# A mixture of experts in items of 32 tokens on four column tiles, and three serial chains of other stages taken apart

## The chip, the cores and the metric

The kernel runs on one core of a Trainium2 chip. The metric is the time of one execution on the device, in microseconds (us); lower is better. All data is float32.

Words used here: PE is TensorE (PEld its weight loads), DVE is VectorE, ACT is ScalarE, POOL is GpSimd, SP is SyncE, which here only issues transfers (DMA). A *bank* is one of the eight accumulators of TensorE, 128 rows of 512 float32. A *column tile* is a strip of TensorE's columns that works on a stationary matrix of 64 or 32 columns and writes its own rows of a bank; two strips of 64 or four of 32 lie side by side.

## What is computed

Three networks in a row, on 256 tokens of width 1024. The part of most interest here is the mixture of experts at the end of the first. Each token goes to 4 of 32 experts; every expert has three matrices of 1024 x 1024 (gate, up and down, 4 MB each):

```python
def moe(h, w_router, b_router, w_gate, b_gate, w_up, b_up, w_down, b_down):
...
    top_logit, top_idx = lax.top_k(logits, TOP_K)
    gates = jax.nn.softmax(top_logit, axis=-1)
...
    def expert_block(args):
        xb, e = args
        g = jnp.minimum(xb @ w_gate[e] + b_gate[e], SWIGLU_LIMIT)
        u = jnp.clip(xb @ w_up[e] + b_up[e], -SWIGLU_LIMIT, SWIGLU_LIMIT)
        act = g * jax.nn.sigmoid(SWIGLU_ALPHA * g) * (u + 1)
        return act @ w_down[e] + b_down[e]
```

The reference's router gives the experts, on the inputs used, these numbers of tokens: 24, 33, 24, 34, 36, 4, 13, 32, 47, 47, 52, 21, 25, 51, 33, 13, 27, 58, 22, 29, 73, 9, 35, 41, 25, 35, 39, 38, 34, 20, 14, 36.

The second network is a hybrid layer (three branches, a convolution among them whose channels are layer-normed, and merge gates):

```python
    cv = jax.nn.silu(layer_norm(causal_depthwise_conv(glu, conv_w, conv_b), cv_ln_g, cv_ln_b))
...
    gates = jax.nn.sigmoid(merge.reshape(B, S, N_BRANCH, D))
```

The third has two layers of feed-forward network, mixer (a pooling in one, a differential attention in the other) and feed-forward network. The attention ends in

```python
    o = sweep_query_blocks(block, q)
    o = rms_norm_3(o, subln_g) * (1 - lam_init)
    return o.reshape(b, s, d) @ w_o
```

with `o` of 8 heads of 128.

## The kernel before

Stages follow one another: `mla`, `route`, `experts_tiled` (268 to 1234 us of the span), `second` (to about 1612), and then in `third` the feed-forward networks `ffn`, `pool_mixer`, `ffn`, `ffn`, `diff_attention`, `ffn`, and a last norm. Within a stage every engine has its own instruction list, in the order in which the code is written; semaphores are all that ties them. No scheduler reorders anything.

**Route and experts.** `route` makes a list of *items*: an item is up to `SLOTS` (64) tokens of one expert. `weights_of[e]` is the expert of item e, `ends_of[x]` the number of items up to the end of expert x, `n_items` their sum. Both are read on the chip by `value_load`. An item goes through these steps on PE:

- `gather`: a 0/1 matrix `choice` (token by slot) picks the item's rows out of `h_rows`, into bank X; ACT copies them to `x_rows`; `turn` transposes them back into bank X, and ACT copies that to `xs`, features by slots.
- `gate_up`: `product` takes `xs` as the stationary matrix (128 x 64) and the weights as the moving one (128 x 512), the two halves of the output on two column tiles; gate goes into bank G, up into bank U. ACT copies each to rows (`g_rows`, `u_rows`), `turn` transposes each, DVE adds biases, limits, and multiplies, with a sigmoid of ACT's between, which gives `act_s`.
- `down`: the same product with `act_s`, into bank Y; ACT copies it to `ys`.
- `spreading` and `scatter`: a matrix of gates by slot (`gated`), transposed into `spread`, adds `ys` into the rows of the tokens in banks 0 to 3, which stay open over all items.

The steps of neighbouring items are interleaved: in turn e of the loop PE does gate_up(e), with gather(e+1) in its middle, then spreading and down of e-1, the turns of e+1, and scatter(e-1).

**Weights.** An expert's 12 MB lie in six tiles `raw0` to `raw5` of 2 MB (gate 0 and 1, up 2 and 3, down 4 and 5), of which there is only one set. SP runs through the experts: for each piece it waits until `used[p]` has reached `ends_of[e-1]`, which is when the last item of expert e-1 has gone over the piece, and issues the load (L1411). PE waits for `landed[p]`.

**Second.** `project(n)` is a loop of n turns of the projection of the stage's input by `w_in` (L1795), 64 matmuls a turn; the last three are for the merge gates, and ACT's `take` applies the sigmoid to what it leaves. PE sums the convolution's channels (a product with ones, L1869 for the squares, taken by ACT at L1951), and then attends (L1878, L1805) with the probabilities that ACT copies at L1964.

**SideSums.** Beside each feed-forward network, POOL fetches pieces of the modulation matrix `in_mod_w` and DVE sums them. POOL begins with a memset of `ffn_side_bias` (L337), its load (L333), and two loads of weights (L328). DVE starts the network with the norm's scaling (L437).

**Diff-attention's end.** DVE's `take_o` (L2866) copies head by head into `o` (16 blocks of 128 x 128, the tile `ring`). ACT squares all of `o` (L2800), DVE sums by head (L2885), ACT takes a root, DVE the reciprocal and 16 scalings (L2893), PE transposes (L2745), DVE copies four banks with the gain `subln` (L2898), and PE multiplies by `w_o` (L2755).

## Time and profile before

| | us |
|---|---|
| median of 3 runs | 2725.25 (2723.86 to 2725.43) |
| the profiled execution | 2726.04 |
| its span | 2724.4 |
| PE busy | 2519.5 (92%) |
| DVE, ACT, POOL busy | 1060.0, 369.6, 43.4 |
| moved by DMA | 728 MB, mean 267 GB/s |

The profile comes from one execution. "Busy" is the sum of the times in which an engine had an instruction in work. The *granted clock* is the share of TensorE's full clock that the chip gave it (1.00 is 2.4 GHz, 0.5 is 1.2 GHz). The DMA share is the mean busy share of the core's 16 DMA engines. In the rows below, the number in brackets at the end of a row is the time that the engine had stood before it, and behind the arrow what ended that.

The experts take 965 us, over a third of the time, and in them the DMA share is near 1 for most of the time. In the second and third network PE is busy nearly throughout.

### The profile page before, as it was taken

Reading aid. Unit: us, or ns where it says so; the run is one execution under the profiler, and the core shown is the slowest. Engines: PE = TensorE matmul, PEld = TensorE weight load, DVE = VectorE, ACT = ScalarE, POOL = GpSimd, SP = SyncE. Lnnn points to the kernel's source line nnn. Section 1 sums busy time; section 2 is a strip of 40 time slices with the busy share of each in tenths; the row PEclk is TensorE's granted clock in tenths of the full one; section 3 lists DMA queues with packets and bytes.
Section 4 is the critical chain, followed back from the end, with each engine's and each line's share of the span. In section 5 each row is a group of like instructions: output and inputs, shape, how many; then the busy total and the mean of one; then the engine's idle time right before and its main releaser. Section 6 shows DMA issues by size and latency. Waiting matters only on the chain. (4 is left out here: it accounts for less than half of the span.)

```text
span 2724.4 us, 33615 instructions
## 1 busy us (share of the span) xinstructions
PE 2519.5 (92%) x12943; PEld 1538.4 (56%) x12944; DVE 1060.0 (39%) x2210; ACT 369.6 (14%) x743; POOL 43.4 (2%) x64
## 2 busy tenths in 40 slices
PE   6998999999999799997999889998999999987998
PEld 2444333333333233336878758777876887855876
DVE  1233121121221121224381248746996443244433
ACT  2122111111111111111121210011002000131001
POOL 0000000000000000000000000000100000000000
PEclk8998999999999899998989999999999999998999
DMA  8603999999997799998434359754997553140443
GB/s 330 261 10 138 427 429 428 428 429 428 428 429 334 336 429 429 428 409 315 148 117 158 120 196 347 273 179 141 378 382 273 197 165 108 69 155 26 153 160 102
DMA packets 188019, 728.24 MB, mean 267 GB/s; under 512 B 9758, under 2 KB 103292, under 8 KB 159156
## 3 DMA queue, kind: packets, MB, share of 16 engines
q1 hardware_dynamic: 168324, 651.29, 61.2%
q0 software_dynamic: 19632, 76.09, 7.1%
q8 instruction: 43, 0.70, 0.1%
q14 instruction: 20, 0.16, 0.0%
HBM read 726.30 MB, written 1.05 MB: 267 GB/s over the span
## 5 line engine op out<-in xcount | busy, mean ns | idle before, releaser
L1496 PE MATMUL bank<-experts_raw,experts_xs 128*64 128x512 f32 x2112 | 472.7, 596 | 18.7 <-DMA experts_raw<-in_w_up 15.2
L1496 PEld LDWEIGHTS bank<-experts_raw,experts_xs 128*64 128x64 f32 x2112 | 147.0, 137 | 334.3 <-issue 289.3
L2379 PE MATMUL bank<-big,ffn_actT 128*128 128x512 f32 x704 | 309.1, 592 | 0.0
L1496 PE MATMUL bank<-experts_raw,tiled_act_s 128*64 128x512 f32 x1056 | 241.4, 602 | 52.1 <-DMA experts_raw<-in_w_down 50.8
L1795 PE MATMUL bank<-hT,ring 128*128 128x256 f32 x1024 | 224.7, 383 | 3.2 <-DMA ring<-in_w_in 2.1
L1795 PEld LDWEIGHTS bank<-hT,ring 128*128 128x128 f32 x1024 | 196.6, 192 | 32.1 <-issue 5.0
L2379 PEld LDWEIGHTS bank<-big,ffn_actT 128*128 128x128 f32 x704 | 130.5, 190 | 148.3 <-issue 148.3
L1630 DVE COPY tiled_spread<-bank 128x256 f32<-128x256 f32 x33 | 14.0, 425 | 441.2 <-PE bank L1532 441.2
L1496 PEld LDWEIGHTS bank<-experts_raw,tiled_act_s 128*64 128x64 f32 x1056 | 71.3, 138 | 200.3 <-issue 123.2
L2254 PEld LDWEIGHTS bank<-hT,big 128*128 128x128 f32 x1408 | 165.2, 193 | 18.3 <-issue 18.3
L2254 PE MATMUL bank<-hT,big 128*128 128x128 f32 x1408 | 166.3, 277 | 0.0
L296 DVE SCALAR_TENSOR_TENSOR layer_sums<-ring,cact,layer_sums 128x512 f32 (+1 forms) x210 | 140.5, 747 | 0.8 <-DMA ring<-in_mod_w 0.8
L1661 DVE TENSOR_TENSOR tiled_up<-bank,tiled_cur 128x512 f32<-128x512 f32 x33 | 22.8, 692 | 256.2 <-PE bank L1516 256.2
L2254 PE MATMUL bank<-big,ffn_sums_of_weights 128*128 128x128 f32 x1056 | 121.9, 275 | 0.2 <-DVE ffn_sums_of_weights L2221 0.2
L2254 PE MATMUL bank<-big,ring 128*128 128x128 f32 x1056 | 121.5, 275 | 0.0
L2254 PEld LDWEIGHTS bank<-big,ffn_sums_of_weights 128*128 128x128 f32 x1056 | 119.8, 192 | 0.4 <-issue 0.4
L2254 PEld LDWEIGHTS bank<-big,ring 128*128 128x128 f32 x1056 | 119.7, 192 | 0.0
L2273 DVE TENSOR_TENSOR ring<-ffn_gu,bank 128x256 f32<-128x256 f32 x22 | 9.3, 422 | 226.2 <-PE bank L2254 226.2
L2254 PE MATMUL bank<-big 128*128 128x128 f32 x704 | 85.9, 275 | 0.0
L2439 ACT ACTIVATE ffn_gu<-ffn_gu 128x512 f32<-128x512 f32 x44 | 27.8, 632 | 408.2 <-DVE ffn_gu L2273 408.2
L2254 PEld LDWEIGHTS bank<-big 128*128 128x128 f32 x704 | 82.1, 192 | 0.0
L1542 PE MATMUL bank<-tiled_ys,tiled_spread 64*128 64x512 f32 x264 | 65.6, 615 | 0.8 <-ACT tiled_ys L1586 0.8
(479 smaller groups left out, 2645.1 us busy)
## 6 DMA issues: line engine op xcount, KB each, us to landing
experts_raw<-in_w_gate SPq DMA_DIRECT2D x64, 2048.0 KB, 23.7
experts_raw<-in_w_up SPq DMA_DIRECT2D x64, 2048.0 KB, 25.1
experts_raw<-in_w_down SPq DMA_DIRECT2D x64, 2048.0 KB, 25.5
big<-in_ffn_w_gu SPq DMA_DIRECT2D x88, 1024.0 KB, 9.5
ring<-in_mod_w POOLq DMA_DIRECT2D x30, 2048.0 KB, 10.8
big<-in_ffn_w_down SPq DMA_DIRECT2D x44, 1024.0 KB, 5.1
ring<-in_w_in SPq DMA_DIRECT2D x16, 2048.0 KB, 8.5
mla_wm<-in_w_mod SPq DMA_DIRECT2D x24, 1024.0 KB, 6.7
```

The source lines that it names most:

```text
L296: op = vec.scalar_tensor_tensor(dst[:, o], src[:, j, o], c[:, j:j + 1], dst[:, o], ALU.mult, ALU.add)
L1496: last = nc.tensor.matmul(bank[b][h * HALF:(h + 1) * HALF, :], stationary(kt), raw[p][:, k, h * C:(h + 1) * C], start=kt == 0, stop=kt == ...
L1542: op = nc.tensor.matmul(bank[2 * t + h][:], spread[rows, t * P:(t + 1) * P], ys[rows, :], start=False, stop=end)
L1630: vec.tensor_copy(spread[:], bank[X][:, 0:SEQ]).then_inc(spread_ready, 1)
L1661: vec.tensor_tensor(tiles(up), turned(U), wide(cur[:, KT:2 * KT]), ALU.add).then_inc(u_taken, 1)
L1795: last = nc.tensor.matmul(bank[b][:, (f % 2) * SEQ:(f % 2 + 1) * SEQ], w_k[s][:, k, f * P:(f + 1) * P], core.hT[:, k, :], start=k == 0, st ...
L2254: last = self.nc.tensor.matmul(core.bank[b][:, o:o + P], left(m, k), right(k), start=k == 0, stop=k == half - 1)
L2273: op = lambda o, x, y, f=ALU.add: vec.tensor_tensor(o, x, y, f)
L2379: last = nc.tensor.matmul(bank[b][:], actT[:, s, f, t * P:(t + 1) * P], wd[:, s, f, n * 512:(n + 1) * 512], start=start and f == 0, stop=s ...
L2439: nc.scalar.activation(gu[:, :, 0, :], gu[:, :, 0, :], ACT.Silu).then_inc(*silu_ready.up())
```

## The change

The number of slots in an item falls from 64 to 32, and four strips of TensorE's columns are used in place of two. Gate and up of one item now share bank G (gate's two halves and up's two halves are its four quarters), so one copy of ACT (`gu_rows`) and one `turn_gu` serve both. In `down` two strips take the even k and two the odd k of each half; the two partial sums lie in different rows of `ys`, and are added by `scatter`, whose matrix `gated` has each slot's gate twice. `gate_up` is called in halves of its k, and the order of the steps in the loop changes; the pieces are loaded in the order 0, 2, 1, 3, 4, 5. `route` counts up to eight items for an expert (columns of the table `row`) and clears the upper half of `x_rows` on POOL.

Outside the experts: in `second`, `project(3)` becomes `project(2)` before and `project(1)` behind the sums of L1869, and ACT's sigmoids are split in the same way. In `SideSums.gpsimd` the first two loads of weights go ahead of the memset, which waits for the network's norm. In `diff_attention` squares and sums are taken for heads 0 to 5 first and for 6 and 7 later; the scalings go by quarters of two heads, each of which frees PE's transposes; ACT makes the copies of DVE; and PE's product waits for each pair of features apart.

```diff
-SLOTS = 64
+SLOTS = 32
...
+        for s in range(2):
+            load(s, slice(self.first * PIECE, (self.first + 1) * PIECE))
+        if ready:
+            pool.wait_ge(*ready)
         if self.bias is not None:
             self.st.nc.gpsimd.memset(self.bias[:], 0.0).then_inc(*self.zeroed.up())
             pool.wait_ge(*self.zeroed.own())
         load_bias(slice(self.first * PIECE, (self.first + 1) * PIECE))
...
+    GATE_UP, DOWN = (0, 2, 1, 3), (4, 5)
...
-            load(1, 0)
-            load(1, 1)
-            with sp.Fori(2, E) as e:
-                load(e, 0)
-                load(e, 1)
-                load(e - 1, 2)
-            load(E - 1, 2)
+                for p in pieces:
+                    sp.wait_ge(used[p], last)
+                    weights.load(sp, which, p)
+
+            with sp.Fori(1, E) as e:
+                load(e, weights.GATE_UP + weights.DOWN)
...
+            def gate_up(e, *halves):
+                if 0 in halves:
+                    after(pe, xs_ready, e)
+                    after(pe, gu_copied, e)
+                expert = expert_at(pe, e)
+                for q in halves:
+                    for m in range(2):
+                        pe.wait_ge(landed[2 * m + q], 16 * expert + 16)
+                    for k in range(ROWS):
+                        kt = ROWS * q + k
+                        for m in range(2):
+                            for h in range(2):
+                                o = (2 * m + h) * SLOTS
+                                last = nc.tensor.matmul(bank[G][o:o + SLOTS, :], tiles(xs)[:, kt % 4, kt // 4, :],
+                                                        raw[2 * m + q][:, k, h * C:(h + 1) * C],
+                                                        start=kt == 0, stop=kt == KT - 1)
+                            if k == ROWS - 1:
+                                last.then_inc(used[2 * m + q], 1)
+
+            def down(e):
+                after(pe, act_ready, e + 1)
+                expert = expert_at(pe, e)
+                for q in range(2):
+                    pe.wait_ge(landed[4 + q], 16 * expert + 16)
                     for k in range(ROWS):
                         kt = ROWS * q + k
                         for h in range(2):
...
+                            o = (2 * h + k % 2) * SLOTS
+                            last = nc.tensor.matmul(bank[Y][o:o + SLOTS, :], tiles(act_s)[:, kt % 4, kt // 4, :],
+                                                    raw[4 + q][:, k, h * C:(h + 1) * C],
+                                                    start=kt < 2, stop=kt >= KT - 2)
+                    last.then_inc(used[4 + q], 1)
+
+            def turn_gu(e):
+                after(pe, gu_copied, e + 1)
                 after(pe, u_taken, e)
                 for j in range(4):
...
+                    last = nc.tensor.transpose(bank[T][:, j * P:(j + 1) * P], gu_rows[:, adjacent(j)], core.ident[:])
+                last.then_inc(gu_turned, 1)
...
             with pe.Fori(1, items) as e:
-                gate_up(e)
-                turn(e + 1, g_rows, g_copied, G, g_turned)
+
+                gate_up(e, 0)
+                down(e - 1)
+                gather(e + 1)
+                gate_up(e, 1)
                 spreading(e - 1, x_copied, e + 1)
-                down(e - 1)
+                turn_gu(e)
                 after(pe, spread_ready, e)
-                turn(e + 1, x_rows, x_copied, X, x_turned)
-                turn(e + 1, u_rows, u_copied, U, u_turned)
+                turn_x(e + 1)
                 scatter(e - 1)
...
             with act.Fori(1, items) as e:
+                take_y(e - 1)
                 take_gu(e)
-                take_y(e - 1)
...
-            project(3)
+            project(2)
             pe.wait_ge(*S["squared"].next(pe))
             core.claim(pe, 6)
             for j in range(4):
                 last = nc.tensor.matmul(bank[6][:, 0:SEQ], core.ones[:], glu[:, j, 0:SEQ],
                                         start=j == 0, stop=j == 3)
             last.then_inc(*core.filled[6].up())
+            project(1)
...
-            take(MERGE, 3, ACT.Sigmoid)
+            take(MERGE, 1, ACT.Sigmoid)
             act.wait_ge(*S["centred"].next(act, 4))
             run(glu[:, :, 0:SEQ], tiles(B_GLU), ACT.Square).then_inc(*S["squared"].up())
+            take(MERGE + 8, 1, ACT.Sigmoid)
             act.wait_ge(*S["chan_var"].next(act))
             run(chan[:, 0, :], chan[:, 1, :], ACT.Sqrt).then_inc(*S["chan_dev"].up())
             for j in range(4):
                 act.wait_ge(*S["scaled"].next(act))
                 run(tiles(B_GLU)[:, j, :], tiles(B_GLU)[:, j, :], ACT.Silu, scale=core.column("cv_ln_g_2", j),
                     bias=core.column("cv_ln_b_2", j)).then_inc(*S["cv_ready"].up())
+            take(MERGE + 16, 1, ACT.Sigmoid)
...
-                side.gpsimd(pool)
+                side.gpsimd(pool, norm.normed.next(pool, TT))
...
-            pe.wait_ge(*S["o_ready"].next(pe))
             for q in range(4):
+                pe.wait_ge(*S["o_ready"].next(pe))
...
+                        if b == 0 and k % 2 == 0:
+                            core.copied(pe, k // 2)
...
+            def squares(first, end):
+
+                for b in (6, 7):
+                    act.wait_ge(*core.emptied[b].ahead(TT + end // 2))
+                heads = slice(first * P, end * P)
+                run(junk[:, :, heads], o[:, :, heads], ACT.Square).then_inc(*S["o_sq"].up())
...
+                if h == H3 - 2:
+                    squares(0, H3 - 2)
             core.load_root(act)
-            act.wait_ge(*S["mixed"].next(act))
-            run(junk, o, ACT.Square).then_inc(*S["o_sq"].up())
+            squares(H3 - 2, H3)
...
+            for q in range(4):
+                core.filled[q].passed(act, 4)
+                act.wait_ge(*core.filled[q].next(act))
+                run(oT[:, 2 * q:2 * q + 2, :], bank[q][:].rearrange("p (f n) -> p f n", f=2), ACT.Copy, scale=subln[:])\
+                    .then_inc(*core.emptied[q].up())
...
+            sums(0, H3 - 2)
             take_o(H3 - 2)
             take_o(H3 - 1)
-            dve.wait_ge(*core.read(dve, 6))
-            dve.wait_ge(*core.read(dve, 7))
-            vec.tensor_copy(lam[:, 6:7], lam[:, 5:6]).then_inc(*S["mixed"].up())
-
-            dve.wait_ge(*S["o_sq"].next(dve))
-            heads = lambda a: a.rearrange("p t (h n) -> p t h n", h=H3)
-            then(vec.reduce_sum(ostat[:, 0, :].rearrange("p (t h) -> p t h", t=TT), heads(junk), AX))
+            sums(H3 - 2, H3)
+            for b in (6, 7):
+                dve.wait_ge(*core.read(dve, b))
             vec.tensor_scalar(ostat[:, 1, :], ostat[:, 0, :], 1.0 / P, RMS_EPS, ALU.mult, ALU.add)\
                 .then_inc(*S["o_mean"].up())
             dve.wait_ge(*S["o_root"].next(dve))
             then(vec.reciprocal(ostat[:, 3, :], ostat[:, 2, :]))
-            for t in range(TT):
-                for h in range(H3):
-                    i = t * H3 + h
-                    op = vec.tensor_scalar(o[:, t, h * P:(h + 1) * P], o[:, t, h * P:(h + 1) * P],
-                                           ostat[:, 3, i:i + 1], None, ALU.mult)
-            op.then_inc(*S["o_ready"].up())
             for q in range(4):
-                dve.wait_ge(*core.filled[q].next(dve))
-                vec.tensor_scalar(oT[:, 2 * q:2 * q + 2, :], bank[q][:].rearrange("p (f n) -> p f n", f=2),
-                                  subln[:], None, ALU.mult).then_inc(*core.emptied[q].up())
+                for h in (2 * q, 2 * q + 1):
+                    for t in range(TT):
+                        i = t * H3 + h
+                        op = vec.tensor_scalar(o[:, t, h * P:(h + 1) * P], o[:, t, h * P:(h + 1) * P],
+                                               ostat[:, 3, i:i + 1], None, ALU.mult)
+                op.then_inc(*S["o_ready"].up())
+                core.filled[q].passed(dve, 1)
```

Left out of the diff are the widths of tiles and tables that follow from `SLOTS`, the bank numbers, the code that `gate_up` and `down` replace, and the wait `mixed`, which is gone.

**PE's list, the loop over the items.** In the order's rows, `experts_xs` is `xs`, `experts_raw` the weights, TENSOR_LOAD and ISA belong to the reading of the item's expert. Before, from the gather in the middle of gate_up to the end of the turn:

```order
L1524 MATMUL bank<-experts_h_rows,experts_choice 64x512 x4
L1496 MATMUL bank<-experts_raw,experts_xs 64x512 x16
L1516 MATMUL bank<-ident,tiled_g_rows 128x128 x4
L1532 MATMUL bank<-ident,tiled_gated 128x128 x2
L1462 ISA
L1462 TENSOR_LOAD experts_weights_of
L1462 ISA x2
L1492 ISA
L1496 MATMUL bank<-experts_raw,tiled_act_s 64x512 x16
L1516 MATMUL bank<-ident,experts_x_rows 128x128 x4
L1516 MATMUL bank<-ident,tiled_u_rows 128x128 x4
L1542 MATMUL bank<-tiled_ys,tiled_spread 128x512 x4
```

After, from down(e-1) on, which now stands between the two halves of gate_up(e) (the first half is above these rows):

```order
L1522 ISA
L1527 MATMUL bank<-experts_raw,tiled_act_s 32x512 x16
L1468 REGISTER_ALU
L1550 MATMUL bank<-experts_h_rows,experts_choice 32x512 x4
L1475 TENSOR_LOAD experts_weights_of
L1475 ISA x2
L1506 ISA
L1512 MATMUL bank<-experts_raw,experts_xs 32x512 x16
L1558 MATMUL bank<-ident,tiled_gated 128x128 x2
L1536 MATMUL bank<-ident,tiled_gu_rows 128x128 x4
L1542 MATMUL bank<-ident,experts_x_rows 128x128 x4
L1568 MATMUL bank<-tiled_ys,tiled_spread 128x512 x4
```

Down(e-1) and the gather moved ahead of gate_up's second half, the turns of g and u became one, and spreading, turns and scatter are all that stands between the end of an item's gate_up and the next one's.

**SP's list, one turn of the loop over the experts.** Before, from the last gate piece on (the waits' registers are loaded by TENSOR_LOAD):

```order
L1411 DMA experts_raw<-in_w_gate 128x4096
L1469 TENSOR_LOAD experts_ends_of
L1469 ISA x2
L1411 DMA experts_raw<-in_w_up 128x4096 x2
L1469 ISA
L1469 TENSOR_LOAD experts_ends_of
L1469 ISA x2
L1411 ISA
L1411 DMA experts_raw<-in_w_down 128x4096
L1411 ISA
L1411 DMA experts_raw<-in_w_down 128x4096
```

After, the whole turn:

```order
L1491 ISA
L1482 TENSOR_LOAD experts_ends_of
L1482 ISA x2
L1425 ISA
L1425 DMA experts_raw<-in_w_gate 128x4096
L1425 DMA experts_raw<-in_w_up 128x4096
L1425 ISA
L1425 DMA experts_raw<-in_w_gate 128x4096
L1425 DMA experts_raw<-in_w_up 128x4096
L1425 DMA experts_raw<-in_w_down 128x4096 x2
```

Before, the down pieces of an expert were issued behind the gate and up pieces of the next one; now they are issued in their own expert's turn, and `ends_of` is read once a turn in place of three times.

**PE's list, the merge gates in the second network.** Before, from the last matmuls of project(3) on; `second_glu` is the squared convolution, `second_logit` the attention's probabilities:

```order
L1795 MATMUL bank<-hT,ring 128x256 x16
L102 REGISTER_ALU
L102 COMPARE_AND_BRANCH
L1869 MATMUL bank<-second_glu,ones 128x256 x4
L1878 MATMUL bank<-ident,second_logit 128x128 x8
L1805 MATMUL bank<-second_sg,big 128x256 x2
```

After:

```order
L1821 MATMUL bank<-hT,ring 128x256 x16
L102 REGISTER_ALU
L102 COMPARE_AND_BRANCH
L1895 MATMUL bank<-second_glu,ones 128x256 x4
L102 UNCONDITIONAL_BRANCH
L1821 MATMUL bank<-hT,ring 128x256 x64
L102 REGISTER_ALU
L102 COMPARE_AND_BRANCH
L1905 MATMUL bank<-ident,second_logit 128x128 x8
L1831 MATMUL bank<-second_sg,big 128x256 x2
```

A third of the projection (the row of 64 matmuls, between its branches) moved from ahead of L1869 to behind it, now L1895, and ahead of the first transposes of the attention, now L1905.

## Rows read from the trace of the kernel before

**Rows 1.** Table of windows, the experts' stage; columns in its first line.

```profile
core 0: us, PE busy (x) PEld busy (x) DVE busy (x) ACT busy (x) POOL busy (x), PEclk, DMA share, GB/s
300.00:850.00 550.00, 514.96 (x2404) 182.90 (x2404) 113.02 (x342) 69.39 (x115) 0.00 (x0) 1.00 1.01 428
850.00:900.00 50.00, 33.70 (x160) 11.97 (x156) 7.91 (x23) 4.85 (x8) 0.00 (x0) 0.89 0.72 300
900.00:1000.00 100.00, 98.97 (x458) 36.05 (x460) 21.83 (x67) 12.05 (x20) 0.00 (x0) 0.97 0.86 366
...
1190.00:1235.00 45.00, 38.46 (x176) 13.09 (x172) 9.88 (x25) 6.89 (x14) 0.00 (x0) 1.00 0.97 391
```

**Rows 2.** The page's costliest groups: busy us, mean ns, idle before.

```profile
L1496 PE MATMUL bank<-experts_raw,experts_xs 128*64 128x512 f32 x2112 | 472.7, 596 | 18.7 <-DMA experts_raw<-in_w_up 15.2
...
L2254 PE MATMUL bank<-hT,big 128*128 128x128 f32 x1408 | 166.3, 277 | 0.0
```

**Rows 3.** Timeline (start, us, what), PE, at products on four column tiles.

```profile
73.78 1.92 PE L569 MATMUL bank<-mla_wm,first_cpad 128*32 128x512 f32 x16
75.64 7.17 PE L778 MATMUL bank<-mla_win,mla_ctx_hT 128*128 128x256 f32 x32
```

**Rows 4.** Timeline at expert 20, the one with two items.

```profile
873.18 3.76 SPq L1411 DMA_DIRECT2D experts_raw<-in_w_gate  x2
...
876.26 1.89 PE L1524 MATMUL bank<-experts_h_rows,experts_choice 128*64 128x512 f32 x8
...
877.98 7.04 PE L1496 MATMUL bank<-experts_raw,experts_xs 128*64 128x512 f32 x32
...
901.03 9.36 PE L1496 MATMUL bank<-experts_raw,tiled_act_s 128*64 128x512 f32 x32 [15.12 <-DMA experts_raw<-in_w_down]
...
910.32 0.75 PE L1516 MATMUL bank<-ident,experts_x_rows 128*128 128x128 f32 x4
...
911.48 1.99 PE L1542 MATMUL bank<-tiled_ys,tiled_spread 64*128 64x512 f32 x8
...
913.40 7.09 PE L1496 MATMUL bank<-experts_raw,experts_xs 128*64 128x512 f32 x32
```

**Rows 5.** Transfers, KB each and us to landing: issued 873 to 874; whole span.

```profile
experts_raw<-in_w_gate SPq DMA_DIRECT2D x1, 2048.0 KB, 8.3
...
experts_raw<-in_w_down SPq DMA_DIRECT2D x64, 2048.0 KB, 25.5
```

**Rows 6.** Timeline, the end of the experts.

```profile
1227.68 3.65 PE L1496 MATMUL bank<-experts_raw,tiled_act_s 128*64 128x512 f32 x16 [1.33 <-DMA experts_raw<-in_w_down]
...
1232.12 1.99 PE L1542 MATMUL bank<-tiled_ys,tiled_spread 64*128 64x512 f32 x8 [0.79 <-ACT tiled_ys L1586]
```

**Rows 7.** Second network: the projection's group, then the timeline at its two waits.

```profile
L1795 PE MATMUL bank<-hT,ring 128*128 128x256 f32 x1024 | 224.7, 383 | 3.2 <-DMA ring<-in_w_in 2.1
...
1514.61 1.99 PE L1869 MATMUL bank<-second_glu,ones 128*128 128x256 f32 x8 [2.03 <-ACT second_glu L1951]
...
1522.60 2.07 PE L1805 MATMUL bank<-second_sg,big 128*128 128x256 f32 x4 [5.12 <-ACT second_sg L1964]
```

**Rows 8.** Timeline at the start of two feed-forward networks.

```profile
1613.50 2.51 DVE L437 TENSOR_SCALAR big<-x,ffn_small 128x1024 f32<-128x1024 f32 x2
1613.84 0.97 POOL L337 MEMSET ffn_side_bias<- 128x1024 f32 x1
...
2497.83 1.42 DVE L437 TENSOR_SCALAR big<-x,ffn_small 128x1024 f32<-128x1024 f32 x2
```

**Rows 9.** Timeline, the end of the differential attention.

```profile
2453.31 0.42 DVE L2866 COPY ring<-bank 128x256 f32<-128x256 f32 x1 [0.47 <-PE bank L2724]
...
2455.97 2.29 DVE L2885 TENSOR_REDUCE diff_ostat<-diff_weights_wqk 128x16 f32<-128x2048 f32 x1 [1.98 <-ACT diff_weights_wqk L2800]
...
2459.03 3.22 DVE L2893 TENSOR_SCALAR ring<-ring,diff_ostat 128x128 f32<-128x128 f32 x16
2462.31 3.52 PE L2745 MATMUL bank<-ident,ring 128*128 128x128 f32 x16 [9.04 <-DVE ring L2893]
...
2466.99 3.24 PE L2755 MATMUL bank<-diff_weights_wqk,hT 128*128 128x512 f32 x7 [1.15 <-DVE hT L2898]
```

More of the change, by code:

```diff
@@ L339, in gpsimd @@
         load_bias(slice(self.first * PIECE, (self.first + 1) * PIECE))
-        for s in range(2):
-            load(s, slice(self.first * PIECE, (self.first + 1) * PIECE))
         with turns(pool, self.n_pieces - 1, *[(x, 1) for x in self.loads + self.w_used]) as i:
@@ L1308, in _ @@
             act.wait_ge(*core.filled[7].next(act))
-            run(item.xs[:], core.bank[7][:], ACT.Copy).then_inc(*core.emptied[7].up())
+            run(item.xs[:].rearrange("p (j c) -> p j c", j=4), item.rows_of(core.bank[7]), ACT.Copy).then_inc(*core.emptied[7].up())
         @block.vector
```

140 lines of the change are left out of this document (64 added, 76 removed).

## Prediction

> **What bounds the kernel now.** The profiled execution took 2726.04 us (span 2724.4); the median of the runs shown is 2725.25, so a sum made on the profiled one stands 0.8 us high, which I leave in. I read first the table of windows over the experts. From 300 to 850 the DMA share is 1.01 at 428 GB/s, with PE busy 515 of 550 us [rows 1]: the transfers of the experts' weights set the pace, and PE fits in under them. One 2 MB piece at 429 GB/s takes 4.89 us, an expert's six take 29.35. The share falls in two places: 300 and 366 GB/s in 850 to 1000, which is (1 - 300/429) x 50 + (1 - 366/429) x 100 = 15.0 + 14.7 us of flow lost, and 391 in the last window, 4.0 us [rows 1]. **33.7 us of flow are lost in all.** So every change to the experts has to be read as lost flow, not as PE time. The timeline around 870 to 925 says why. That expert (number 20, 73 tokens) is the only one with two items of 64 slots. A piece is loaded again only when the expert's last item has used it, so from 873.18 the queue starts empty and the first piece lands 8.3 us after its issue, against some 25 in the steady stream [rows 4, 5]: 8.27 - 4.89 = 3.4 us of start, and PE then stood 15.12 us for the down weights [rows 4].
>
> With one item of about 26.6 us (three products of 32 matmuls, 7.04 to 7.09 us each, a gather of 1.89, three turns of up to 0.75 and a scatter of 1.99 [rows 4], which overlap by a tenth or two where they meet) against 29.35 us of flow, PE waits 2 to 3 us per expert. That is all a faster item can find there, and it isn't on the path.
>
> **Part 1, the experts: the items.** From the reference's routing the tokens per expert are known; in items of 64 that is 33, which the 2112 matmuls of L1496 for gate and up confirm (64 an item [rows 2]). In items of 32 it is **50: 15 experts of one item, 16 of two, one of three.** What is an exception before, the expert whose weights may only be reloaded after a second pass, becomes every second expert. This is what I cost.
>
> *An item's PE time.* Four column tiles in place of two: if the four run together, a product of 64 matmuls takes the time that 32 instructions take now. L1496 goes at 7.04 us per 16 steps of two halves, 0.43 us a step. Four tiles of 32 columns exist at L569: 16 instructions in 1.92 us, the next group starting 1.86 later [rows 3], 0.43 to 0.46 us for each four. So gate and up together 2 x 3.43 us (two steps of four for each of the eight k, halved by piece pairs), down 3.43, gather 1.7, spread 0.4, two turns 0.6 each, scatter 1.9 (the rows of [rows 4] less the overlap), with about 0.9 of waiting for ACT's one copy of gate and up (0.60 us of copy and its signals) and no work between to hide it: **16.0 us against 26.6.** The last stretch, spread, wait, turns and scatter, is 4.1 of them.
>
> *One-item experts.* 16.0 us of PE against 29.35 of flow: PE now stands for about 12 us in each, and they stay at the pace of the DMA. The one cost I see is the clock. After the 15.12 us of standing, the next 32 matmuls took 9.36 us instead of 7.04 [rows 4], and the granted clock of that window is 0.89 instead of 1.00 [rows 1]: 11 us at half clock (1.2 GHz against 2.4). In the new order down(e-1) stands behind gate_up(e, 0), so the down pieces are handed back only 3.4 + 3.4 us after p0 and p2 of the next expert land; the flow of p1 and p3, 9.78 us, covers 9.78 - 3.38 of start - 0.4 of issue - 5.15 until the first half of down is through = 0.85 us. Half clock takes 2.3 us more (9.36 - 7.04), and about 1.4 lie open: **15 x 1.4 = 20.6 us (from 0 to 21).**
>
> *Two-item experts.* The loop that closes is: the second item's gate_up first half ends and gives p0 and p2 back; SP issues (0.4); the queue being empty by then, p0 lands after 8.27 [rows 5]; p2, p1, p3 follow at 4.89 each; the next expert's gate_up second half runs (3.43), its tail (4.1), and the second item's first half again (3.43). 0.4 + 8.27 + 14.68 + 3.43 + 4.1 + 3.43 = 34.3 us, 34.2 with the overlaps of the issue. That is **4.84 over 29.35** where two-item experts follow each other, 4.43 where they follow a one-item expert; 15 that aren't the last of the row, 69.7 us. The two down pieces are issued within that time and land by 33.1 of the 34.3, so they don't lengthen it; they are why the queue is empty when p0 is asked for. The three-item expert adds a whole item, 16.0 + 4.5 = 20.5.
>
> *Sum.* Lost flow 69.7 + 20.6 + 20.5 = 110.8, against 33.7 before: +77.1. After the last piece lands, before: 1227.68 to about 1234, 6.3 us (the 3.65 us of down and a scatter of 1.99 [rows 6]). After, expert 31 has two items, and the last piece can land only before the first's down: half a down, gather, gate_up second half, tail, then down of the second and its scatter (1.7 + 1.7 + 3.4 + 4.1 + 3.4 + 0.8 for the copy + 2.0 = 17.1), with 2.3 for half clock and some 0.5 where PE reads the expert's number: about 19.9, or +13.6. I take **+90.4** for the experts (90.7 by these terms, less the 0.3 of narrower copies in route).
>
> Both ends of what the trace doesn't show: the step of a quad is 0.43 by L569 in runs of 16; in runs of 16 steps back to back no row shows it. The nearest row on short instructions is L2254, 1408 in 166.3 us [rows 2], 0.118 us for each pair of weight load and matmul, so 0.47 us for four pairs against 0.43: a tenth more on 13 us of an item gives 1.3 us, of which the loop holds 6.9 us' worth of matmul (0.69) and the tail some: +16 in all. I keep 0.43, since the nearest row in form is L569, and carry the 16 as an end. From an empty queue the landing took 8.27; between 7.5 and 9.0, 16 restarts move the sum from 70 to 105. The switches between tile shapes get fewer, less than 0.2 us an item.
>
> [...]
>
> **Part 2, outside the experts.** *Second:* the merge gate's projection is cut in three and laid into the waits of its chain. PE waited 2.03 us before L1869 and 5.12 before L1805, for ACT's square and for the copy behind its table loads and Silus [rows 7]. Now ACT squares after the first of three sigmoids, while PE is at the second third of the projection, and the last third, 64 matmuls of 0.22 us or 14 us [rows 7], stands where PE waited 5.12. It was done anyway, and covers either wait. ACT changes its table more often, beside those projections. I take 7.4: 2.03 + 5.12, and 0.25 for the half clock that a wait of 5 us leaves behind (L1805's first four in 2.07 us [rows 7]), from 6 to 9. *SideSums:* the bias memset waits for the norm, so L437 at 1613.50 no longer shares its port: 2.51 us for two against 1.42 at 2497.83 [rows 8]: 1.1 us, once, since only here a memset of 0.97 fell on it. Behind the waiting memset on POOL stand the bias load and the later turns of weights, not the first two, which now go ahead of it; the bias, which VectorE needs with the first weights, comes a microsecond or two later and is small beside their 2 MB. *Diff-attention:* from the end of the last copy, 2453.73, to the first L2755 at 2466.99 there are 13.3 us [rows 9]: a square over all heads (about 1.9), a reduction of 2.29, 16 scalings of 3.22, 16 transposes of 3.52, four copies that end 0.4 before. After: a quarter of square and sum (0.5 + 0.65), root and reciprocal (0.8), then scalings, transposes and ACT copies in four interleaved quarters, the scalings setting the pace at 0.8 each, L2755 after the first two quarters. It starts at about 2460.6, 6.4 earlier, but waits once more per pair of banks and begins at the low clock: **5 (3.4 to 6.5).** Sum of part 2: 7.4 + 1.1 + 5.0 = **13.5 less (9 to 16).**
>
> **Forecast:** 2726.0 + 90.4 - 13.5 = 2802.9, **2803 us.**
>
> **The rivals.** *A, half clock costs nothing.* For: the products are half as long, so the half clock may be over sooner for each, and 0.85 us are covered. Against: 9.36 in place of 7.04 after one wait [rows 4]. 2803 - 20.6 = 2782. *B, slower quads.* Four tiles in long runs at 0.47 us, by L2254's pace: 2803 + 16 = 2819; for it, a quad in 0.43 us leaves 0.107 for each weight load with its matmul, and L2254 takes 0.118 [rows 2]; against it, L569 does it, in runs of 16 [rows 3]. *C, the other side: the loads never run dry.* If SP's issue for p0 comes while p5 is still in flight, the 3.4 of start are hidden, and if the loop closes in 29.35, two-item experts cost nothing. Then 2726.0 - 33.7 + 20.5 + 13.6 - 13.5 = 2713, faster by 13. It decides from 29.35: my loop has 34.3, and 30.9 even with the start hidden, so PE's share of it (10.96 us) would have to be under 9.4 as well. For: each of the loop's terms has been timed elsewhere than in such a loop, and most could only come out shorter. Against: at 873.18 it did start empty [rows 4, 5]. *D, the change doesn't do what it says:* quads that run as pairs make an item 26.5 us and two-item experts 53 us; over 3100. L569 speaks against it [rows 3].
>
> **How the numbers follow.** Forecast 0.60 (2790 to 2815, its unknown landing time and part 2), A 0.13, B 0.17, C 0.05, D 0.02, the remaining 0.03 for a loss I haven't seen that stops at about 2730. The range takes in A and B with the ends of the landing time: **2772 to 2832.** A measurement of this kernel can tell about 0.2% (5.5 us). Faster by more: C, 0.05. Within: 0.02. Slower: 0.93.
>
> **What would show it.** In the profile after: items in x50; DMA share 1.0 over a row of one-item experts and about 0.86 (29.35/34.2) over two-item experts; gate loads landing 8 to 9 us after issue in the latter; PE's largest idle group under L1512 waiting for gate or up, some 12 us an expert, with PEclk at 0.8 or 0.9 across the stage; the experts' last scatter about 90 us later. L569's pace in L1512: 16 matmuls in 1.9 us. In second no wait over 1 us before L1895 and L1831; in diff-attention L2785 some 6 us after the last copy. I'm wrong if the DMA share stays at 1.0 over two-item experts (C), if the loop's length isn't 34 us, or if PEclk stays at 1.0 with the one-item experts at 29.35 (A).

## The result

The changed kernel takes **2803.96 us** (median of 4 runs, 2799.70 to 2808.41), the kernel before 2724.56 (4 runs, 2722.70 to 2725.43): a ratio of **1.0294, with an interval of 1.0276 to 1.0313**. That is 79.4 us slower, where 2803 was forecast. The profiled execution of the changed kernel took 2799.7 us, 73.7 more than the profiled one of before (2726.04).

The table of windows of the changed kernel, columns as in [rows 1], for the long stretch of the experts, for two one-item experts (434 to 495) and for one expert of two items that follows another such (537 to 572):

```profile
300.00:1190.00 890.00, 695.70 (x5178) 295.27 (x5170) 195.68 (x765) 105.75 (x214) 0.00 (x0) 0.91 0.91 377
```

```profile
537.00:572.00 35.00, 32.31 (x255) 14.92 (x251) 9.18 (x36) 4.95 (x10) 0.00 (x0) 1.00 0.86 360
...
434.00:495.00 61.00, 35.36 (x248) 14.51 (x250) 9.17 (x36) 4.64 (x10) 0.00 (x0) 0.78 0.99 413
```

[Rows 1] had a DMA share of 1.01 nearly everywhere and 0.72 to 0.86 around one expert. Now the mean is 0.91, 0.86 wherever two-item experts follow each other, and near 1 over one-item experts, where instead the granted clock fell to 0.78. The costliest groups and the transfers, from the page (columns as in [rows 2] and [rows 5]):

```profile
L1512 PE MATMUL bank<-experts_raw,experts_xs 128*32 128x512 f32 x3200 | 423.6, 638 | 220.9 <-DMA experts_raw<-in_w_up 216.8
...
L1527 PE MATMUL bank<-experts_raw,tiled_act_s 128*32 128x512 f32 x1600 | 183.7, 592 | 0.5 <-issue 0.5
...
experts_raw<-in_w_gate SPq DMA_DIRECT2D x64, 2048.0 KB, 9.9
```

3200 matmuls of gate and up at 64 an item are the 50 items. TensorE is busy less than before (2436.7 us against 2519.5), though it does half as many items again. It waits instead: 220.9 us ahead of gate and up (L1512) and 0.5 ahead of down (L1527). Before, it waited 18.7 us ahead of gate and up [rows 2] and 52.1 ahead of down, whose row in the page of before is

```profile
L1496 PE MATMUL bank<-experts_raw,tiled_act_s 128*64 128x512 f32 x1056 | 241.4, 602 | 52.1 <-DMA experts_raw<-in_w_down 50.8
```

A gate piece lands 9.9 us after its issue in the median, where it was 23.7 on the page of before. That median mixes two cases. Behind a two-item expert the first gate piece lands after 8.0 to 8.5 us and the second after 9.2 to 10.1: the queue had run dry. Behind a one-item expert the same pieces take 14.4 to 22.5 us, since others are still in flight.

**One two-item loop.** Timeline of the changed kernel, PE and SP, start and duration first; L1512 is gate and up, L1527 down, L1568 the scatter:

```profile
537.73 0.34 SPq L1425 DMA_DIRECT2D experts_raw<-in_w_gate  x1
...
550.89 3.64 PE L1512 MATMUL bank<-experts_raw,experts_xs 128*32 128x512 f32 x32 [0.86 <-DMA experts_raw<-in_w_up]
554.32 3.64 PE L1527 MATMUL bank<-experts_raw,tiled_act_s 128*32 128x512 f32 x32
556.31 2.05 SPq L1425 DMA_DIRECT2D experts_raw<-in_w_down  x2
...
560.67 3.64 PE L1512 MATMUL bank<-experts_raw,experts_xs 128*32 128x512 f32 x32 [1.00 <-DMA experts_raw<-in_w_up]
...
566.21 1.99 PE L1568 MATMUL bank<-tiled_ys,tiled_spread 64*128 64x512 f32 x8
568.28 3.73 PE L1512 MATMUL bank<-experts_raw,experts_xs 128*32 128x512 f32 x32
...
572.15 0.34 SPq L1425 DMA_DIRECT2D experts_raw<-in_w_gate  x1
```

This is the loop of the prediction, term by term. The gate piece is asked for at 537.73; the first half can run from 550.89, 13.2 us later (8.27 + 4.89 had been put for that); down hands its pieces back at 556.31; the second half waits for p1 and p3 until 560.67; the tail follows, and the second item's first half at 568.28, whose end lets SP ask for the next gate piece at 572.15. From 537.73 to 572.15 there are **34.4 us, where 34.2 to 34.3 was forecast** and the flow of six pieces takes 29.35. Over the eight places where two-item experts of the row follow each other the mean is 34.5.

**One one-item expert:**

```profile
440.21 1.99 PE L1568 MATMUL bank<-tiled_ys,tiled_spread 64*128 64x512 f32 x8
454.26 5.64 PE L1512 MATMUL bank<-experts_raw,experts_xs 128*32 128x512 f32 x32 [12.06 <-DMA experts_raw<-in_w_up]
459.66 3.67 PE L1527 MATMUL bank<-experts_raw,tiled_act_s 128*32 128x512 f32 x32
461.67 2.05 SPq L1425 DMA_DIRECT2D experts_raw<-in_w_down  x2
```

PE stands 12.06 us, as forecast, and the next 32 matmuls take 5.64 us where 3.64 are usual: 2.0 us of half clock, and by so much later come the down pieces' issues.

**Where the 73.7 us of the two profiled executions lie.** The experts' last scatter ends at 1328.0 against 1234.1 [rows 6]: **+93.9**. Counted from the stage's own start it is more. The first gate piece was asked for at 243.2 us here and at 248.6 in the trace of before, so from that issue to the last scatter there are 1084.8 us against 985.5, **+99.3**; this start lies between 241.2 and 250.3 in five traces of kernels whose code is the same up to there. Laying the starts of the same matmuls of both traces side by side shows the rest: the first projections of the second network have 4.6 less, though nothing of them was changed (they have 5.4 to 6.3 less than the trace of before in e3, e4 and e5 too, which leave that network as it was); from the end of the projections to the stage's product 9.0 less; the start of the next network 1.0; the differential attention about 6. The end of the experts:

```profile
1321.58 3.64 PE L1527 MATMUL bank<-experts_raw,tiled_act_s 128*32 128x512 f32 x32 [0.48 <-issue]
1326.03 1.99 PE L1568 MATMUL bank<-tiled_ys,tiled_spread 64*128 64x512 f32 x8 [0.80 <-ACT tiled_ys L1615]
```

The last piece of the weights landed at 1307.1, so the tail behind it is 20.9 us, against 6.5 (1227.6 to 1234.1).

**The second network and the attention after.** To be read beside [rows 7] and [rows 9]:

```profile
1573.92 1.89 PE L1895 MATMUL bank<-second_glu,ones 128*128 128x256 f32 x8
...
1575.65 27.79 PE L1821 MATMUL bank<-hT,ring 128*128 128x256 f32 x128
...
1604.91 1.13 PE L1831 MATMUL bank<-second_sg,big 128*128 128x256 f32 x4 [0.60 <-ACT second_sg L1993]
```

The waits of 2.03 and 5.12 us are 0 and 0.60, and the first four of L1831 take 1.13 us where they took 2.07. (The row x128 covers 64 matmuls of the code: each is two in the trace, so this third of the projection is 27.8 us, not the 14 that the prediction gives; its cover was more than enough in either case.)

```profile
2532.61 0.76 DVE L2908 COPY ring<-bank 128x256 f32<-128x256 f32 x2
...
2535.59 3.23 DVE L2939 TENSOR_SCALAR ring<-ring,diff_ostat 128x128 f32<-128x128 f32 x16
2536.51 3.60 PE L2774 MATMUL bank<-ident,ring 128*128 128x128 f32 x16 [4.03 <-DVE ring L2939]
...
2539.91 5.54 PE L2785 MATMUL bank<-diff_weights_wqk,hT 128*128 128x512 f32 x12
```

From the end of the last copy (2533.37) to the product with `w_o` there are 6.5 us where [rows 9] had 13.3: PE's transposes now begin 0.9 us after the first scaling. Up to the end of that product there are 34.4 us against 41.0.

### The profile page after: what moved, and what is told of

It reads as the page before. It is cut to its first block and busy times, and to the rows that moved or that the text cites. A ratio compares the mean times of both kernels' runs of the same rounds, so it can differ in the third digit from the quotient of the medians.

```text
span 2798.0 us, 38712 instructions
## 1 busy us (share of the span) xinstructions
PE 2436.7 (87%) x14885; PEld 1557.6 (56%) x14886; DVE 1089.4 (39%) x2512; ACT 375.1 (13%) x799; POOL 43.5 (2%) x65
## 5 line engine op out<-in xcount | busy, mean ns | idle before, releaser
L1512 PE MATMUL bank<-experts_raw,experts_xs 128*32 128x512 f32 x3200 | 423.6, 638 | 220.9 <-DMA experts_raw<-in_w_up 216.8
L1512 PEld LDWEIGHTS bank<-experts_raw,experts_xs 128*32 128x32 f32 x3200 | 146.5, 116 | 464.6 <-issue 457.7
L1657 DVE COPY tiled_spread<-bank 128x256 f32<-128x256 f32 x50 | 21.2, 425 | 728.5 <-PE bank L1558 728.5
L1527 PE MATMUL bank<-experts_raw,tiled_act_s 128*32 128x512 f32 x1600 | 183.7, 592 | 0.5 <-issue 0.5
L2283 PEld LDWEIGHTS bank<-hT,big 128*128 128x128 f32 x1408 | 164.7, 193 | 18.7 <-issue 18.7
L1527 PEld LDWEIGHTS bank<-experts_raw,tiled_act_s 128*32 128x32 f32 x1600 | 73.1, 110 | 98.6 <-issue 93.2
L1615 ACT ACTIVATE tiled_ys<-bank 128x512 f32<-128x512 f32 x50 | 29.9, 597 | 634.4 <-PE bank L1527 634.4
L1568 PE MATMUL bank<-tiled_ys,tiled_spread 64*128 64x512 f32 x400 | 99.4, 615 | 0.8 <-ACT tiled_ys L1615 0.8
L1550 PE MATMUL bank<-experts_h_rows,experts_choice 128*32 128x512 f32 x400 | 96.7, 592 | 0.0
```

What stands on the lines that cost most here:

```text
L1512: last = nc.tensor.matmul(bank[G][o:o + SLOTS, :], tiles(xs)[:, kt % 4, kt // 4, :], raw[2 * m + q][:, k, h * C:(h + 1) * C], start=kt == ...
L1527: last = nc.tensor.matmul(bank[Y][o:o + SLOTS, :], tiles(act_s)[:, kt % 4, kt // 4, :], raw[4 + q][:, k, h * C:(h + 1) * C], start=kt < 2, ...
L1550: last = nc.tensor.matmul(bank[X][n * SLOTS:(n + 1) * SLOTS, :], choice[:, t, :], h_rows[:, t, n * C:(n + 1) * C], start=t == 0, stop=t == ...
L1568: op = nc.tensor.matmul(bank[2 * t + h][:], spread[rows, t * P:(t + 1) * P], ys[rows, :], start=False, stop=end)
L1615: run(ys[:], bank[Y][:], ACT.Copy).then_inc(y_copied, 1)
L1657: vec.tensor_copy(spread[:], bank[X][:, 0:SEQ]).then_inc(spread_ready, 1)
```

## Experiments

Each ratio is to the kernel before, run on the same chip in the same session. Medians of the kernel before were 2722.20, 2724.14 and 2721.62 us in the three sessions.

### The parts alone

The first four kernels are the kernel before with some hunks of the diff and nothing of the experts; e5 is the other half.

**e1: the three chains.** The hunks of `SideSums.gpsimd`, `second` and `diff_attention`.

> The kernel before with the three chains taken apart and nothing of the experts. Theory: 13.5 us less than before (9 to 16), 2711. In the profile of the changed kernel the second network gave 9.0 us, the memset 1.0 and the differential attention 6.0 (its first matmuls against those of before), 16.0 together, so 2708 to 2711. Rival, that the outside gains come from another phase of the clock after a longer experts' stage and not from the edits: 0 to 5 less.

Measured: 2703.80 us, ratio 0.9929 (0.9912 to 0.9947), 18.4 us less in the median, 14 to 24 by the interval. Inside its trace, the second network's part gives 8.6, the start of the next network 1.0 and the attention 4.9, 14.5 together, so the rival of 0 to 5 is out. Its span is 22.3 us below that of the trace of before; the rest of this lies ahead of the edits, where stages differ by some us from run to run. It is the fastest of all kernels with the whole computation here.

**e2: the second network's chain.** `project(3)` cut, sigmoids split.

> The kernel before with the merge gates' projection cut in three, alone. Theory: both waits, 2.03 and 5.12 us, go, and some of the half clock behind them: 7.4 less, up to 9.0. Rival: ACT's additional table loads and the later copy take back a part: under 5 less.

Measured: 2711.74, ratio 0.9953 (0.9935 to 0.9971): 8 to 18 us by the interval. Its own trace has 8.9 us gained between the projections and L1897. So the waits go and nothing comes back from ACT's additional table loads; the term was too small, not wrong in kind. What was missing is the half clock, which had held not only the first four of L1805 but the transposes and products up to 1527 (2.07, 1.06 and 1.80 us in the trace of before; 1.13, 0.60 and 1.03 in the changed kernel's): some 2 us where 0.25 were put.

**e3: the attention's end.** Squares and sums in two parts, scalings by quarters, copies on ACT.

> The kernel before with the differential attention's end by quarters, alone. Theory: 5 less (3.4 to 6.5); the changed kernel's trace shows 6.0, of which 1.3 lie ahead of the edit. Rival: the low clock eats it: 2 to 3 less.

Measured: 2716.77, ratio 0.9976 (0.9964 to 0.9988), 5.4 us in the median, 3 to 10 by the interval. Timeline of its run:

```profile
2455.54 3.23 DVE L2910 TENSOR_SCALAR ring<-ring,diff_ostat 128x128 f32<-128x128 f32 x16
...
2456.47 3.68 PE L2745 MATMUL bank<-ident,ring 128*128 128x128 f32 x16 [4.03 <-DVE ring L2910]
...
2459.94 2.37 PE L2756 MATMUL bank<-diff_weights_wqk,hT 128*128 128x512 f32 x3
```

The same picture as in the changed kernel. From the last copy to the end of the product with `w_o` there are 35.2 us against 41.0, 5.8 less: the term of 5 stands, within its range.

**e4: the memset.** Two loads first, then the wait for the norm, then the memset.

> The kernel before with POOL's two weight loads ahead of the bias and the memset waiting for the norm, alone. Theory: 1.1 less. Rival: nothing, since the memset now falls on DVE's next steps: 0.

Measured: 2722.46, ratio 1.0003 (0.9991 to 1.0014): no change that can be told. The instruction itself did what was said:

```profile
1600.88 1.63 DVE L439 TENSOR_SCALAR big<-x,ffn_small 128x1024 f32<-128x1024 f32 x2
1601.22 1.60 POOL L328 DMA_DIRECT2D ring<-in_mod_w  x2
...
1602.81 0.97 POOL L341 MEMSET ffn_side_bias<- 128x1024 f32 x1
```

The two scalings take 1.63 us in place of 2.51 [rows 8], 0.9 less, since the memset comes after them. It reaches PE, whose transposes wait for the scalings; first the trace of before, then that of e4, where the window cuts the row off after six:

```profile
1615.50 3.65 PE L467 MATMUL bank<-ident,big 128*128 128x128 f32 x16 [10.16 <-DVE big L437]
```

```profile
1601.87 1.51 PE L469 MATMUL bank<-ident,big 128*128 128x128 f32 x6 [9.15 <-DVE big L439]
```

The first down product of the network still begins 1.0 us earlier against the end of the stage before it (110.1 us behind it, not 111.0), so the rival, that the memset then costs as much in VectorE's next steps, isn't borne out in this trace. The interval of the ratio (about 3 us to either side) is wider than 1 us, so the gain in the total isn't shown.

**e5: the experts alone.** All other hunks.

> The changed experts and route alone, the three chains as before. Theory: 90.4 us more than before, 2815 (the profile of the changed kernel has 93.9 at the end of the experts, 2818). Rival, that part of the 90 is paid by the outside gains' place: under 2808.

Measured: 2819.89, ratio 1.0347 (1.0329 to 1.0365), 95.7 us more in the median, 90 to 99 by the interval. All its runs lie above the rival's 2808. With e1 it adds up: 95.7 - 18.4 = 77.3 against 79.4 measured for the whole. The experts' part is paid in full; the other part only hides a fifth of it. Its trace has 1087.3 us from the first gate issue to the last scatter, where the six traces with the experts as before have 984.6 to 986.4. By the stage's own length the experts thus cost 98 to 103 us, somewhat more than the medians of the totals give; no run here settles why.

### What in the experts costs

**e6: one item for every expert.**

```diff
-    over = np.arange(SEQ // SLOTS) * SLOTS - (np.arange(SEQ // SLOTS) == 0)
+    over = np.where(np.arange(SEQ // SLOTS) == 0, -1, 1e6)
```

> The changed kernel, but every expert gets one item: tokens beyond an expert's 32nd are left out (18 items fewer). Theory of the loops: no two-item loop is left; 31 experts at 30.7 us in place of 29.35, lost flow 43, end of the experts at 1240 in place of 1328, the whole 2716. Rival, slower for another reason than second items (quads, the order, the waits): the end at 1290 or later. If the half clock costs nothing: 1199, the whole 2675.

Measured: 2714.38 us (ratio 0.9974); the experts end at 1240.6 where 1240 was forecast. With the second and third items out and everything else of the change in, 89.6 us of the changed kernel are gone. The quads, the copy of gate and up in one, the new order and the longer wait ahead of `turn_gu` are thus not what makes it slow: second items are. And the experts' stage is still 7.5 us longer than in the kernel before (993.0 us from the first gate issue to the last scatter, against 985.5), though it has one item less than that one. The table of windows tells why (columns as in [rows 1]), first of e6:

```profile
300.00:1190.00 890.00, 519.87 (x3534) 197.78 (x3530) 132.95 (x522) 71.78 (x145) 0.00 (x0) 0.78 0.98 409
```

Each expert takes 30.7 us in the mean, at a granted clock of 0.78 over the whole stage. At one of them:

```profile
447.15 5.76 PE L1512 MATMUL bank<-experts_raw,experts_xs 128*32 128x512 f32 x32 [12.62 <-DMA experts_raw<-in_w_up]
...
454.69 2.05 SPq L1425 DMA_DIRECT2D experts_raw<-in_w_down  x2
```

**e7: the same with TensorE kept busy.**

```diff
                 scatter(e - 1)
+                for i in range(12):
+                    nc.tensor.matmul(bank[Y][:], core.ident[:], h_rows[:, 0, 0:C], start=True, stop=True)
```

> As the run before it (tokens beyond the 32nd left out), with 12 matmuls of 128x512 on a free bank after each scatter, 10.3 us, in the time in which PE waits for weights. Theory: PE's clock stays up, the bubble of 1.4 us per expert goes, and more work makes it 30 to 40 us faster than the run without them: about 1209 at the end of the experts, 2686. Rival, the bubble is a matter of order and latency and not of the clock: no change, or slower.

Measured: 2683.84 us, 30.5 less than e6, from more work. The windows of e7, and its timeline at one expert (L1597 is the added work):

```profile
300.00:1190.00 890.00, 803.16 (x4434) 368.70 (x4426) 140.33 (x549) 76.07 (x154) 0.00 (x0) 1.00 1.01 428
```

```profile
426.33 10.57 PE L1597 MATMUL bank<-experts_h_rows,ident 128*128 128x512 f32 x24
438.45 3.77 PE L1512 MATMUL bank<-experts_raw,experts_xs 128*32 128x512 f32 x32 [1.55 <-DMA experts_raw<-in_w_up]
441.88 3.77 PE L1527 MATMUL bank<-experts_raw,tiled_act_s 128*32 128x512 f32 x32
443.99 2.05 SPq L1425 DMA_DIRECT2D experts_raw<-in_w_down  x2
```

The clock is 1.00, the DMA share 1.01, each expert takes 29.4 us, which is the pure flow, and the experts end at 1207.4. Against e6: the down pieces are asked for 5.5 us after the first half begins (438.45 to 443.99) and not 7.5 (447.15 to 454.69). So the 1.3 to 1.4 us per one-item expert are the half clock's, as the prediction had it, and rival A, by which it costs nothing, is out. It is the one place of the case where work added to the busiest engine made the kernel faster.

**e8: more work in every item of the changed kernel.** The same edit with `range(3)`, all 50 items in.

> The changed kernel with 3 such matmuls, 2.6 us, behind each of the 50 scatters. By the theory an item's tail counts once in each loop of a two-item expert, twice in the three-item expert and at the end, and not in one-item experts: 55 more (16 or 17 x 2.6, and some two-item experts fall back to PE's own pace of 37). Rival, every item counts: 50 x 2.6 = 130 more. Rival, the DMA sets the pace: 0 to 10 more.

Measured: 2863.67, 59.7 more than the changed kernel; 55 was expected, against 130 if every item counted and 0 to 10 if none did. Timeline of SP in its run, at the place of the same two-item expert as above:

```profile
554.60 0.34 SPq L1425 DMA_DIRECT2D experts_raw<-in_w_gate  x1
...
575.03 2.05 SPq L1425 DMA_DIRECT2D experts_raw<-in_w_down  x2
...
592.25 0.34 SPq L1425 DMA_DIRECT2D experts_raw<-in_w_gate  x1
```

The loop is 37.65 us, 3.2 more than 34.4 for 2.6 us added; a one-item expert behind another takes 30.6 to 30.9, no longer than in the changed kernel. An item's tail counts once in a two-item loop and not at all in a one-item expert. The 0.6 us beyond the 2.6 are PE's own pace: in this loop PE is busy 36.87 of 37.65 us, and all eight two-item experts behind another take 37.6. Two items of 16.2 us, with 2.6 added to each, give that.

**e9: down after both halves.**

```diff
-                gate_up(e, 0)
+                gate_up(e, 0, 1)
                 down(e - 1)
                 gather(e + 1)
-                gate_up(e, 1)
```

> The changed kernel with one step moved: both halves of gate_up(e) run before down(e-1), so the down pieces are handed back only after the next expert's last gate and up pieces have landed and been used. Theory: now every expert pays, the one-item ones too, since no flow covers the issue and the start of the down pieces: some 5.1 us of PE more ahead of their release plus 3.8 of issue and start, less 0.85 of cover; 32 x 7.7 = 247 us more than the changed kernel, about 3050. Rival, only the two-item experts' loop counts: 16 x 5.1 = 80 more, 2885. Rival, the split order brings nothing: 2804.

Measured: 3076.52, 272.6 more than the changed kernel, where 247 was expected and the rivals gave 80 and 0. Timeline at a one-item expert:

```profile
543.58 5.93 PE L1512 MATMUL bank<-experts_raw,experts_xs 128*32 128x512 f32 x32 [15.26 <-DMA experts_raw<-in_w_up]
553.34 6.12 PE L1512 MATMUL bank<-experts_raw,experts_xs 128*32 128x512 f32 x32 [3.83 <-DMA experts_raw<-in_w_up]
559.28 3.62 PE L1527 MATMUL bank<-experts_raw,tiled_act_s 128*32 128x512 f32 x32
561.24 2.05 SPq L1425 DMA_DIRECT2D experts_raw<-in_w_down  x2
```

Down's pieces are asked for 17.7 us after the first half begins, not 7.4. By then all of gate and up has landed and the queue has run dry in one-item experts too: behind another such they take 39.8 to 40.7 us, and two-item ones behind a two-item one 41.8 to 43.2. The latter are 7.7 us longer than in the changed kernel (42.2 against 34.5 in the mean), as expected; the former 9.1 (40.1 against 31.1). In the one-item expert above the low clock catches both halves (5.93 and 6.12 us where 3.64 are usual), while the expectation put this way at the full clock. That this makes the difference is argued, not shown: in a two-item expert the second half is slow as well (5.18 us at 637.15). Of the 25 us that it missed, 18 lie in the experts' stage, which is 265 us longer; the rest lies outside it, where traces differ by as much anyway. The split of gate_up, with down between the halves, is what the change can't do without once a set of weights has one buffer.

### Is there more in keeping the clock up?

**e10: e1 with work ahead of the norms' transposes.**

```diff
+        if self.normalise:
+            for i in range(12):
+                nc.tensor.matmul(core.bank[0][:, 0:P], core.ident[:], core.ident[:], start=True, stop=True)
```

> The kernel with the three chains alone (e1), and 12 matmuls of 128x128 of the identity on a free bank ahead of each norm's transposes, where PE otherwise stands 3 to 9 us. If what e7 showed in the experts holds here, the transposes and the first products after them run at the full clock: 1 to 2 us at each of 8 norms, 8 to 16 less than e1's ratio of 0.993, so 0.987 to 0.990. Rival, these waits are too short or the 3 to 6 us of added work end after the norm is ready: 0 to 10 more, 0.993 to 0.997.

Measured: 2714.41, ratio 0.9979 (0.9963 to 0.9995), 0.005 above e1's ratio: the rival's side, and even past its end. The two timelines, first of e1:

```profile
1597.98 3.64 PE L469 MATMUL bank<-ident,big 128*128 128x128 f32 x16 [9.14 <-DVE big L439]
```

and of e10:

```profile
1600.35 5.09 PE L465 MATMUL bank<-ident 128*128 128x128 f32 x24 [7.78 <-PEq L155]
1605.29 0.93 PE L472 MATMUL bank<-ident,big 128*128 128x128 f32 x7
```

The transposes do run at the full clock (all 16 take 1.91 us in place of 3.64; the window cuts the row off after seven), but the added work is itself done at the half clock and takes 5.09 us. Of the 9.14 us that PE stands there 7.78 lie ahead of the barrier between the stages, where nothing of the new stage can be put, and at the later norms 2.76 of 4.04. So the last transpose ends 14.6 us behind the work before it, against 12.8 in e1; at the norm of `route` and at the later ones it ends between 0.3 us earlier and 2.1 later than in e1. e7 had 12 us to fill, in which the added work was through before the weights landed; here it wasn't. That added work in these waits brings nothing is shown. Where the whole loss of some 11 to 14 us lies isn't: behind the experts the two traces are equally long (1473.8 us in e10, 1474.5 in e1), and e1 and e10 ran in different sessions.

## Why the prediction was right

*What sets the pace.* That the experts are to be read as lost flow held: e6 took the second items out and with them 89.6 us, and e7 the rest of the stage's loss by the clock; e8 made every item longer and only the two-item loops paid.

*The two-item loop.* Forecast 34.2 us, measured 34.4 for one and 34.5 in the mean. Each term is in the timeline above. An item's PE time was put at 16.0 us, though the terms listed for it add up to 16.4; e8's loops give 16.2.

*Four column tiles.* 32 matmuls of L1512 in 3.64 us, the next group starting 3.43 after, as L569's 16 in 1.92 said [rows 3]. Rival B (0.47 us a quad) and rival D (quads as pairs) are out. The trace has 3.43 us for 8 quads, 0.43 each.

*Half clock.* Forecast 1.4 us for a one-item expert, 20.6 together (15 x 1.4 is 21.0). Measured 30.7 us an expert in e6 and 29.4 in e7, 1.3 to 1.4 each; in the changed kernel itself, the one-item experts behind another take 30.5 to 31.6, 31.1 in the mean.

*The tail.* Forecast +13.6, measured 20.9 - 6.5 = +14.4. The sum is near, its terms less so:

```profile
1308.05 3.64 PE L1527 MATMUL bank<-experts_raw,tiled_act_s 128*32 128x512 f32 x32
```

The last piece had landed at 1307.1, ahead of the whole first down and not in its middle, and the 2.3 us of half clock that the sum has there don't show: this down and the last one both take 3.64 us.

*The experts' sum.* Forecast +90.4; +93.9 by the end of the experts in the profiled executions, 95.7 by e5, and +99.3 by the stage's own length. In the last of these, the time from the first gate issue to the last landing grew by 84.8 us (979.1 to 1063.9) where +77.1 was put, and the tail by 0.8 more than put. Some 0.3 us in each two-item loop and as much in each one-item expert are of that size.

*Outside.* Forecast 13.5 less, within 9 to 16; measured 18.4 (14 to 24) by e1, and 14.5 to 16 inside the traces. The term that was mis-sized is the second network's: 7.4 put, 8.6 to 9.0 in three traces, for the half clock it left out. The working of that term also had the moved third of the projection at 14 us, by counting 64 matmuls of the code at the trace's duration for one of two; it is 27.8, and changed nothing, since the wait that it covers is 5.12. The attention's 5 holds (5.4 in e3, 5.8 and 6.5 inside two traces). The memset's 1.1 shows as 0.9 in the instruction and 1.0 in PE's wait, and can't be told in the total.

*Two errors that cancelled.* The experts cost 3 to 12 us more than forecast, by the measure taken (ends, medians or the stage's own length), and the chains brought 1 to 5 more. The total of 2804 against 2803 is thus nearer than the parts are: the mechanism was right, the last few us are luck.

*Rival C*, by which the queue never runs dry, is out by the landings: 8.1 us for the gate piece issued at 537.73.

## What to carry to other kernels

When weights have one buffer each and are handed back by the last user, count the users of each set before making the unit of work smaller: every set with a second user turns its reload into issue + start + flow + the compute around it. A faster inner loop shortens only the last of these: here 11.0 us of the 34.3, which would have to fall under 6.0 for the loop to close in the flow's 29.35 (an estimate from the prediction's sum, not run). Read the loss from the transfers' side (share, time from issue to landing), and TensorE's busy time as cover only. An engine that waits longer than before may also run slower afterwards; put added work there only where the wait is long and already begun, and where that work ends before what is waited for.

## What the runs showed of the hardware beyond that

- Twelve added matmuls in a wait of 12 us raised the granted clock of the whole stage from 0.78 to 1.00 and took 30.5 us off the kernel (e6, e7). The same idea in waits of which 1.3 to 1.4 us were left brought nothing: the ratio was 0.005 worse, 11 to 14 us (e1, e10).
- A transfer of 2 MB issued to an empty queue landed after 8.0 to 8.5 us behind every two-item and the three-item expert of the changed kernel.
- The kernel before had medians from 2721.6 to 2724.6 over four sessions and single runs from 2711 to 2730. The stages ahead of the experts alone moved their end by 9 us between traces of kernels that are the same up to there (gate's first issue at 248.6 in the trace of before, at 241.2 in e4, at 250.3 in e2), and the first projections of the second network by 6, while the experts' stage itself stayed within 984.6 to 986.4 us in six traces. A change of 1 us can't be told in such a total; it can in the row of its instruction.
